# The QKV entry by token halves: slices of 512 tokens, product rows among the transposes, first weights loaded among x

## What is computed

```python
def rmsnorm(x, g):
    xf = x.astype(jnp.float32)
    y = xf * lax.rsqrt(jnp.mean(xf * xf, axis=-1, keepdims=True) + EPS)
    return (y * g.astype(jnp.float32)).astype(x.dtype)
...
    for i in range(DEPTH):                       # DEPTH = 2
        hn = rmsnorm(h, attn_norm[i])
        qkv = hn @ w_qkv[i]                      # (1024, 1024) @ (1024, 2304)
        ya = sliding_window_sink_attention(...)
        yb = chunked_relpos_attention(..., b_rel_bias[i])
        h = h + jnp.concatenate([ya, yb], axis=-1) @ w_o[i]
        h = h + conv_gated_mlp(rmsnorm(h, ffn_norm[i]), w_up[i], conv_w[i], conv_b[i], w_down[i])
        gate = jax.nn.sigmoid(rmsnorm(h, ple_norm[i]) @ w_ple_gate[i])
        h = h + (p[i] @ w_ple_proj[i]) * gate
```

## Time and profile before

| | |
|---|---|
| median of 3 runs | 2552.94 us (2552.73 to 2553.4) |
| profiled execution | 2553.14 us |
| its span | 2551.3 us |
| TensorE busy | 2514.2 us, 99% of the span |
| VectorE, ScalarE, GpSimd busy | 1376.9, 1308.2, 1016.6 us |
| mean granted TensorE clock | 0.999 |

### The profile page before, as it was taken

The page is one execution under the profiler, slowest core; times in us unless marked ns, Lnnn a source line. Parts: engine busy times, 40 slices in busy tenths (PEclk is TensorE's granted clock), DMA queues, the critical chain, the costliest instruction groups (busy, mean ns, idle before and its releaser), DMA issues.

```text
span 2551.3 us, 41875 instructions
## 1 busy us (share of the span) xinstructions
PE 2514.2 (99%) x13328; PEld 2190.3 (86%) x13328; DVE 1376.9 (54%) x2073; ACT 1308.2 (51%) x2190; POOL 1016.6 (40%) x749
## 2 busy tenths in 40 slices
PE   8999999999999999999999999999999999999999
PEld 7999998877888888888899999988788888888887
DVE  3114666176566568873241146752766566687733
ACT  4335776175555554344353367752755555543342
POOL 3354221238787760001124452201388788500011
PEclk9999999999999999999999999999999999999999
DMA  4111000323333348431111110003232432584312
GB/s 156 49 49 38 21 13 10 99 67 101 101 107 105 96 151 296 140 110 43 38 45 43 50 36 28 2 18 104 68 109 81 120 107 87 175 286 128 100 50 83
DMA packets 179770, 223.85 MB, mean 88 GB/s; under 512 B 7952, under 2 KB 110736, under 8 KB 179632
## 3 DMA queue, kind: packets, MB, share of 16 engines
q1 hardware_dynamic: 179040, 219.66, 27.0%
q0 software_dynamic: 592, 2.46, 0.3%
HBM read 169.08 MB, written 55.36 MB: 88 GB/s over the span
## 4 chain that ended last, share of the span: by engine, by line
PE 93%; DVE 2%; issue 2%; ACT 1%; POOL 1%; DMA 0%; ACTq 0%; DVEq 0%; SPq 0%; POOLq 0%
PE ps L2046 10%; PE ps L2048 10%; PE ps L2047 10%; PE ps L2410 10%; PE ps L2413 10%; PE ps L2412 10%; PE ps L2255 6%; PE ps L2434 5%; PE ps L2436 5%; PE ps L2435 5%; PE ps L2206 3%; PE ps L2236 3%; PE ps L2181 2%; PE ps L2085 1%; DMA h<-in_x 0%
## 5 line engine op out<-in xcount | busy, mean ns | idle before, releaser
L824 POOL TENSOR_TENSOR w_hl<-w_raw,w_hl 128x1024 fp32r<-128x1024 f32 x84 | 201.2, 2395 | 1007.9 <-ACT w_hl L999 1007.9
L2046 PE MATMUL ps<-w_hl,xT 128*128 128x384 f32 (+1 forms) x1280 | 459.2, 359 | 1.2 <-DVE xT L1525 1.1
L2048 PE MATMUL ps<-w_hl,xT 128*128 128x384 f32 (+1 forms) x1280 | 456.1, 356 | 0.0
L2047 PE MATMUL ps<-w_hl,xT 128*128 128x384 f32 (+1 forms) x1280 | 455.9, 356 | 0.0
L999 ACT ACTIVATE w_hl<-w_raw 128x1024 fp32r<-128x1024 f32 x84 | 89.1, 1061 | 423.4 <-PE ps L2048 397.2
L2046 PEld LDWEIGHTS ps<-w_hl,xT 128*128 128x128 f32 x1280 | 240.3, 188 | 22.2 <-DVE xT L1525 2.8
L2048 PEld LDWEIGHTS ps<-w_hl,xT 128*128 128x128 f32 x1280 | 240.3, 188 | 20.3
L2047 PEld LDWEIGHTS ps<-w_hl,xT 128*128 128x128 f32 x1280 | 240.4, 188 | 19.0
L1542 DVE TENSOR_REDUCE q_sum<-sq 128x384 f32 x80 | 44.2, 553 | 271.1 <-ACT sq L1055 271.1
L1854 DVE SCALAR_TENSOR_TENSOR ps<-c_up,ccols,ps 128x1023 f32<-128x1023 f32 x84 | 107.7, 1283 | 151.4 <-ACT ps L1309 151.4
L1115 ACT ACTIVATE probs<-scores,neg_max 128x192 f32<-128x192 f32 (+5 forms) x256 | 144.3, 565 | 36.1 <-DVE neg_max L1614 35.5
(11 more groups left out here) (271 smaller groups left out, 6251.5 us busy)
## 6 DMA issues: line engine op xcount, KB each, us to landing
ad_raw<-v_rows SPq DMA_DIRECT2D x70, 512.0 KB, 3.7
raw_a<-in_w_up SPq DMA_DIRECT2D x44, 512.0 KB, 5.0
raw_g<-in_w_up SPq DMA_DIRECT2D x44, 512.0 KB, 5.1
v_rows<-c_up SPq DMA_DIRECT2D x22, 1024.0 KB, 4.4
w_raw<-in_w_qkv SPq DMA_DIRECT2D x48, 384.0 KB, 3.2
wd_main<-in_w_down SPq DMA_DIRECT2D x30, 512.0 KB, 8.1
v_rows<-hc_g SPq DMA_DIRECT2D x22, 512.0 KB, 5.0
w_raw<-in_w_o SPq DMA_DIRECT2D x16, 512.0 KB, 3.3
```

The source lines that it names most:

```text
L824: nc.gpsimd.tensor_tensor(w_hl[:, slot % 2, 1, :], w_raw[:, slot % 2, :], w_hl[:, slot % 2, 0, :].bitcast(F), ALU.subtract) \
L2046: nc.tensor.matmul(dst, lhs[:, k, 0, cols], wh, start=first, stop=False)
L2047: nc.tensor.matmul(dst, lhs[:, k, 0, cols], wl, start=False, stop=False)
L2048: return nc.tensor.matmul(dst, lhs[:, k, 1, cols], wh, start=False, stop=last)
```

## The change

The first chunk of QKV gets an order of its own on TensorE, `qkv_entry`. The transposes run in 16 slices of 512 tokens (4 token tiles, one k), first all 8 k of the first four tiles and then all 8 k of the other four (`BY_TOKENS`). Product rows of the first four tiles stand between: those of step 0 behind the first 8 slices, those of step 1 among the last 4. The rows of tiles 4 to 7 of steps 0 and 1 follow, and then steps 2 and 3 as before. The chunks 1 to 4 stay in a loop. ScalarE splits weight slot 0 ahead of all slices and slot 1 behind the second slice. SyncE puts weight blocks 0 and 1 behind the first and the second block of x. GpSimd negates the bias table (as 48 x 256 elements in place of 16 x 768), stores it and skews it behind its low parts of slots 2, 3 and 4, and sets the constants behind that of slot 1. The loops over the two layers are written out on SyncE and GpSimd. The counter of slices is 8 larger a layer. VectorE's and ScalarE's order behind the slices is unchanged.

```diff
+BY_TOKENS = [(k, half) for half in range(2) for k in range(KT)]
-XFILLS = 7 * KT
+XFILLS = 8 * KT
...
+        def first_bank(n):
+
+            return ps[:, n if n < TT else 4 + n % 4, :]
...
             for j in range(TT // 2):
                 sp.dma_start(h[:, 2 * j:2 * j + 2, :], x_rows[:, 2 * j:2 * j + 2, :]).then_inc(x_loaded[j], 16)
+                if j < 2:
+
+                    sp.wait_ge(s_w_low_ready, j + 1)
+                    sp.dma_start(w_raw[:, j, 0:2 * QC].rearrange("p (k n) -> p k n", k=2),
+                                 w_qkv[0:1, 256 * j:256 * j + 256, 0:QC].rearrange("a (k p) n -> p (a k) n", p=P)) \
+                        .then_inc(raw_loaded[j], 16)
...
-            with sp.Fori(0, DEPTH) as L:
+            for L in range(DEPTH):
...
-            with pool.Fori(0, DEPTH) as L:
+            for L in range(DEPTH):
...
-                low(0)
-                with pool.Fori(0, 2) as i:
-                    for j in range(4):
-                        low(j + 1, 4, i)
+                between = {1: set_consts, 2: negate_bias, 3: store_bias, 4: skew_bias} if L == 0 else {}
+                for slot in range(9):
+                    low(slot)
+                    if slot in between:
+                        between[slot]()
...
-                x_high(0, 0, {1: 0, 5: 1}, False)
+                high(0)
+                x_high(0, 0, {1: 1}, BY_TOKENS, first_bank)
...
-                x_low(0, 0, False)
+                x_low(0, 0, BY_TOKENS, first_bank)
...
-                pe.wait_ge(s_gate_added, L * 2 * TT + (C_GATE - 2))
-                transpose_x(0, lambda t, k: h[:, t, k * P:(k + 1) * P], every_tile,
-                            ready=lambda t: pe.wait_ge(x_loaded[t // 2], 16))
-
-
-                with pe.Fori(0, QCHUNKS - 1) as i:
-                    row_chunk(0, 4, i, QC,
-                              lambda t: pe.wait_ge(s_qkv_copied, L * QCHUNKS * TT + i * TT + (t + 1)), s_qkv_full, 0)
+                    pe.wait_ge(s_gate_added, L * 2 * TT + (C_GATE - 4))
+                    pe.wait_ge(x_loaded[0], 16)
+                    for m in range(4):
+                        transposes(m, (0, 1))
+                    pe.wait_ge(x_loaded[1], 16)
+                    for m in range(4):
+                        transposes(m, (2, 3))
+                    for m in range(4, TT):
+                        transposes(m)
+                    slot_ready(0)
+                    rows(0, 0, 1, 2, 3)
+                    pe.wait_ge(x_loaded[2], 16)
+                    pe.wait_ge(x_loaded[3], 16)
+                    for m in range(TT, TT + 4):
+                        transposes(m)
+                    slot_ready(1)
+                    for t in range(4):
+                        rows(1, t)
+                        transposes(TT + 4 + t)
+                    rows(0, 4, 5, 6, 7)
+                    rows(1, 4, 5, 6, 7)
+                    row_chunk(0, 0, 0, QC, lambda t: None, s_qkv_full, (2, 3))
+
+                qkv_entry()
+                with pe.Fori(1, QCHUNKS - 1) as i:
+                    row_chunk(0, 4, i, QC, lambda t: copied_row(i, t), s_qkv_full)
```

More of the change, by code:

```diff
@@ L380, in entry_bank @@
             return ps[:, 4 + n % 4, :]
-        def slices(halves):
-            return ENTRY if halves else [(k, None) for k in range(KT)]
-        def rows_of(n, k, half):
-            if half is None:
-                return slice(0, SEQ), pair(k)
-            return slice(half * HALF, (half + 1) * HALF), entry_bank(n)
-        def pair(k):
-            return psf[:, (k % 4) * 1024:(k % 4 + 1) * 1024]
+        def first_bank(n):
+            return ps[:, n if n < TT else 4 + n % 4, :]
         def variant(name, sums=False):
@@ L651, in tiled @@
                     return src.rearrange("a (k p) n -> p (a k) n", p=P)
-                with sp.Fori(0, QCHUNKS) as i:
+                for j in range(0 if L else 2, 4):
+                    load(j, 0, 0, rows2(j, QC), tiled(w_qkv[ds(L, 1), 256 * j:256 * j + 256, 0:QC]))
+                with sp.Fori(1, QCHUNKS) as i:
                     for j in range(4):
@@ L1013, in norm_root, with x_high @@
                     nc.scalar.activation(h_rms[:, tiles], h_mean[:, tiles], ACT.Sqrt).then_inc(s_rms_ready, 1)
-                def x_high(first, gain, between={}, halves=True):
-                    for n, (k, half) in enumerate(slices(halves)):
+                def x_high(first, gain, between={}, order=ENTRY, bank=entry_bank):
+                    for n, (k, half) in enumerate(order):
                         act.wait_ge(s_xfill, L * XFILLS + (first + n + 1))
@@ L1517, in norm_squares, with x_low @@
                     dve.wait_ge(s_squares_v, L * TT + (base + TT // 2))
-                def x_low(first, gain, halves=True):
-                    for n, (k, half) in enumerate(slices(halves)):
+                def x_low(first, gain, order=ENTRY, bank=entry_bank):
+                    for n, (k, half) in enumerate(order):
                         dve.wait_ge(s_xhigh, L * XFILLS + (first + n + 1))
                         scale = 1.0 if gain is None else ncols[:, ds(L * 3 * KT + (gain * KT + k), 1)]
-                        rows, source = rows_of(n, k, half)
-                        nc.vector.scalar_tensor_tensor(out=xT[:, k, 1, rows], in0=source, scalar=scale,
+                        rows = slice(half * HALF, (half + 1) * HALF)
+                        nc.vector.scalar_tensor_tensor(out=xT[:, k, 1, rows], in0=bank(n), scalar=scale,
                                                        in1=xT[:, k, 0, rows].bitcast(F), op0=ALU.mult,
                                                        op1=ALU.subtract).then_inc(s_xlow, 1)
-                x_low(0, 0, False)
+                x_low(0, 0, BY_TOKENS, first_bank)
                 for j in range(TT // 2):
@@ L2018, in slot_ready @@
                     pe.wait_ge(s_w_low_ready, L * SLOTS + i * c + (slot + 1 + C_LOW))
-                def transpose_x(first, source, free=None, ready=None):
-                    def one(t, k):
-                        return nc.tensor.transpose(pair(k)[:, t * P:(t + 1) * P], source(t, k), ident[:, :])
-                    early = TT - 2 if ready is not None else 0
-                    for t in range(early):
-                        ready(t)
-                        for k in range(3):
-                            one(t, k)
-                    for k in range(KT):
-                        if k < 4 and free is not None:
-                            free(k)
-                        if k >= 4:
-                            pe.wait_ge(s_xlow, L * XFILLS + (first + k - 4 + 1))
-                        for t in range(early if k < 3 else 0, TT):
-                            if early and k == 0:
-                                ready(t)
-                            last = one(t, k)
-                        last.then_inc(s_xfill, 1)
                 def products(dst, lhs, t, k, w, kk, n, first, last):
```

91 lines of the change are left out of this document (55 added, 36 removed).

## The result

The changed kernel takes 2562.99 us (median of 6 runs, 2561.15 to 2564.65) and the one before, run beside it, 2553.17 us (6 runs, 2552.64 to 2553.55). The ratio is 1.0038 with a 95% interval from 1.0027 to 1.0048: slower by 9.8 us. The forecast was 2560.6 us, slower by 7.7. The profiled execution took 2562.36 us with a span of 2560.6 us, against a span of 2551.3; the mean granted clock is 0.997 in place of 0.999.

What follows compares the result with a forecast made beforehand. TensorE, busy 99% of the span, was taken as the bound. Layer 0 0.0, layer 1 +4.7 and the clock after the stalls +3.0 gave +7.7 us on 2552.94, so 2560.6 us, range 2554 to 2564.

Steps and rivals of the forecast that it cites:

- Layer 1, +4.7: Entry of layer 1: j=2 starts 3.0 us later, plus 1.7 us for products at the lower clock.
- The way from m=15 to slot 2: From the start of the last transpose group to slot 2 ready: 13.6 us, 2.4 for group and `x_low`, then 11.2 of chain.
- Layer 0, 0.0: Entry of layer 0: first product 8 us sooner, but j=2 at 40.8 against 40.80, no gain and no loss.
- The 0.3 us for slow products: Layer 0, first product rows: 0.3 us added for products that may still run at the lower pace, bounds 0 and 2.
- The stall, 4.8: In front of j=2 in each layer: TensorE stands 4.8 us, slot 2 ready at R + 24.8, TensorE through at R + 20.0.
- The clock behind the stalls, 3.0: Start of j=2 in both layers: lower clock after the stall costs 1.5 us twice, +3.0; each between 0 and 2.5.
- Rival 1: Same stall at j=2 but the clock stays up throughout: layer 0 -0.3, layer 1 +3.0, 2555.6 us; chance 0.25.
- Rival 2: No stall at j=2, slot 2 being ready by R + 20.0: faster, 2547.2 us; chance 0.10.
- Rival 3: Layer 0 entry: weights between x blocks delay x's second block 2.5 us instead of 1.0, 2562.1 us; chance 0.10.

Runs made afterwards that it cites:

- busy stall: Changed kernel with 22 matmuls of 384 columns adding zeros to bank 7 put ahead of j=2: 2558.72 us, ratio 1.0019 to the kernel before.
- the first kernel of the experiments: Changed kernel with slot 2 split behind ScalarE's third sum of squares, not `h_rstd`, first chunk pass written out: 2551.93 us, 0.9994 to the kernel before.
- the last: Changed kernel, slot 2 early, layer 1's slot 0 split ahead of layer 0's last gate tiles, ScalarE's and VectorE's layer loops written out: 2545.85 us, 0.997.
- the kernel with both slots early: Changed kernel, slot 2 early, layer 1's slot 0 split among layer 0's last gate tiles, ScalarE's layer loop written out: 2553.14 us, 0.9999.

## Why the prediction was nearly right

- **The mechanism was right.** TensorE waits for `w_hl` at j=2 in both layers. Slot 2 early takes the loss away, and the unchanged kernel with its chain lengthened shows the same loss. TensorE's order was read rightly too: from the first product to the last `x_low` of layer 0 are 13.8 us, where the prediction had 13.6 (in layer 1, with the clock down, 15.1).
- **Layer 1, +4.7: measured +4.6.** The sum is met by terms that are off both ways. The first product starts 6.8 us behind the transposes, where 6.2 were forecast (the terms given add up to 6.0: 1281.71 + 1.05 + 0.09 + 2.38 + 0.1 is 1285.3 and not 1285.5). ScalarE stands 0.65 us at the turn of its loop with no wait to be seen, which the prediction had not counted. The clock fell at the first product, as taken, but cost 1.3 us and not 1.7: the lower level began 0.6 us before the product (1287.9 by the windows). The rows up to m=15 took 11.6 us at full clock, where 11.2 were forecast. The way from m=15 to slot 2 is 0.7 shorter than forecast and gives these back.
- **Layer 0, 0.0: measured -1.0.** The second block of x was at 10.79 (forecast 11.0) and the first product at 15.26 (15.7). The loads ran at the slow pace, 24 transposes in 4.5 us. The sum went by that row, and the clock row of 1.00 does not fit it. The Trainium skill, "TensorE: Matmul & The Clock Gate" (Part 1: The HAM clock gate), says that the array starts throttled; this pace agrees. The 0.3 us for slow products was not there; they ran 0.173 us apart from the third on. This term is not the same each time: in the kernels of the experiments with the same entry those 24 transposes took 4.0 to 5.0 us, so the -1.0 is good to half a us.
- **The stall, 4.8: measured 4.07 and 4.03.** From the start of slice m=15 to slot 2's low part are 12.9 us (26.83 to 39.77), where I had 13.6: a group and its `x_low` take 2.2 and not 2.4, the chain 10.7 and not the 11.2 or 11.1 of the rows before. Of that difference 0.3 us lie between `h_rstd` and ScalarE's split (0.5 us in place of 0.8); why they fell away was not tested.
- **The clock behind the stalls, 3.0: measured 4.3.** This is the term that was sized wrongly. I took 1.5 us a time, with 1.7 as the usual cost, from the one fall in the trace, which lasted 3.4 us. In layer 0 the clock was down from 38.6 to 45.4 by the windows, 6.8 us, of which 5.6 lay on products, and that cost 2.7. In layer 1 it cost 1.65. The bound of 2.5 was too low by a little. The experiments show that no better single figure was to be had: a fall lasted 3.4 or 6.8 us, and in some executions did not come.
- **Left over:** 0 + 4.7 + 3.0 = 7.7 forecast; -1.0 + 4.6 + 4.3 = 7.9 found by the same places, with a span 9.3 longer. Of the difference 0.7 us lies between the end of the low clock in layer 0 and layer 1's transposes, and the rest behind j=2 of layer 1. The waits there differ by tenths (`ring_three` 4.7 against 4.5); no run settled it. That 7.7 and 7.9 lie so near is luck in part: -1.0 in layer 0 and +1.3 for the clock offset each other.
- **Rival 1** (no fall of the clock) fell: the clock fell behind all three waits of the profiled execution. The busy stall shows what a full clock at j=2 would have given, 2558.7, with the fall at the first product of layer 1 in most executions; the four without it took 2555.9 to 2557.2. **Rival 2** (slot 2 in time) did not happen, but it is what the next edit makes. **Rival 3** fell: x came 0.7 us later than before.

What the change could give at best is now readable. It takes no work from TensorE, only idle time: some 2.5 us in layer 1 and the time lost at a low clock there, and 3.5 to 5 us in layer 0 (j=2 at 36.03 in the first kernel of the experiments and at 37.26 in the last, against 40.80). It moves the first products ahead, but the third weight step hangs on a chain that did not move.

## What to carry to other kernels

When work is moved ahead in order to start a bound engine sooner, follow the next thing it needs, not only the first: here the reserve of 1.2 us in front of the third weight step, which no list of waits shows, turned a start 8.8 us sooner (3.7 of them transposes that moved behind it) into a stall of 4 us. Free that chain together with the move: here the split of slot 2 stood behind `h_rstd`, which it does not need. In these kernels two stalls of some 4 us on TensorE cost half as much again by the lower clock that followed (4.3 us on 8.1, and 4.2 on 7.7).

## What the runs showed of the hardware

- **VectorE and GpSimd stop one another on small things too.** `h_mean`, 128x8, took 2.10 us in place of 0.17 beside a low part of GpSimd, and a 128x512 product of VectorE 2.71 and 2.07 in place of 0.69. GpSimd's low part took 3.41 and 3.44 us in place of 2.34 behind a sum of squares of VectorE that had begun 0.06 and 0.04 us sooner. In each of these rows the one that had begun first went on, and the other one was longer by what was left of it.
- **The lower clock lasted 3.4 or 6.8 us in these profiles.** 6.8 us behind the stall in layer 0 of the changed kernel, 3.4 us at both places in layer 1, and 6.8 us at the first of these in the kernel with the busy stall. In the profiles the clock fell behind idle times of TensorE of 2.5 us and more, and not behind those of 1.1 to 2.1 us named above (the waits for x at the start of the program aside, where the clock row does not fit the pace of the loads). By the mean clock of each execution it did not always fall behind those of 3.2 and 3.3 us either.
- **An idle time can be a loop, and its releaser does not tell.** In the kernel with both slots early VectorE began its first `x_low` of layer 1 2.4 us behind the ScalarE tile to which the timeline puts its wait; with the loop over layers written out this falls below 0.1 us. Where the tile itself is late, the turn of the loop costs little: VectorE is idle for 2.79 us there in the first kernel of the experiments, and still for 2.30 us with its loop written out.
